# A PEER expert kernel on one core: gate blocks loaded in four parts, second top 16 over 64 sums, gathered rows summed at the head of a step

## The reference

```python
s = einsum('thpd,hpnd->thpn', q, sub_keys)            # 8 heads, 2 key halves, 128 keys each
sv, si = top_k(s, 16)                                 # first top 16, per token, head and half
cand = sv[:, :, 0, :, None] + sv[:, :, 1, None, :]    # 16 x 16 = 256 sums per token and head
cidx = si[:, :, 0, :, None] * 128 + si[:, :, 1, None, :]
top_s, pos = top_k(cand, 16)                          # second top 16
idx = take_along_axis(cidx, pos); gate = softmax(top_s)
act = gelu(x . u_tab[idx])                            # 128 experts per token (8 heads x 16)
out = sum_k gate * act * v_tab[idx]
```

## Time and profile before

| | |
|---|---|
| median of 3 runs | 4110.21 us (4100.69 to 4113.46) |
| the profiled execution | 4114.83 us, its span 4112.9 us |
| busy in the span | TensorE 3465.9 us (84%), VectorE 2977.0 us (72%), GpSimd 1071.2 us, ScalarE 996.2 us |
| chain that ended last | TensorE 47%, VectorE 20%, DMA 20%, issue 8%, ScalarE 3% |
| DMA | 1268.02 MB, mean 308 GB/s; in the slices of the 128 steps 359 to 414 GB/s, in the last slice 282 GB/s |
| largest groups | L1067 687.1 us, L1079 490.3 + 240.6 us (TensorE); L1686 462.3 + 307.6 us (VectorE) |

### The profile page before, as it was taken

How to read it: one execution, slowest core, us unless ns; L and a number is a source line. 1 busy time by engine, 2 the same in 40 slices (tenths; PEclk the granted TensorE clock), 3 DMA queues, 4 the chain that set the end, 5 groups by cost and what they waited for, 6 DMA issues and landing times.

```text
span 4112.9 us, 32147 instructions
## 1 busy us (share of the span) xinstructions
PE 3465.9 (84%) x9517; PEld 1750.2 (43%) x9517; DVE 2977.0 (72%) x6346; ACT 996.2 (24%) x2518; POOL 1071.2 (26%) x950
## 2 busy tenths in 40 slices
PE   6876899976779778667777698999899988999998
PEld 4336344432343344224445344444444444444443
DVE  1536797847637686798998777887787867876666
ACT  1212321345241111127668111111111111111111
POOL 0000222211213122332320233333233323333331
PEclk9988899987889889888886899999999999999999
DMA  5343665765757788898882899999999999999997
GB/s 201 135 158 134 232 233 212 273 225 208 266 223 276 281 294 318 307 374 329 322 317 107 359 393 383 395 393 402 368 405 392 414 368 363 386 412 390 403 400 282
DMA packets 254837, 1268.02 MB, mean 308 GB/s; under 512 B 24596, under 2 KB 75028, under 8 KB 135622
## 3 DMA queue, kind: packets, MB, share of 16 engines
q0 software_dynamic: 131504, 958.53, 59.1%
q1 hardware_dynamic: 121720, 302.19, 19.7%
q10 hardware_dynamic: 1440, 5.24, 0.3%
HBM read 1216.30 MB, written 49.58 MB: 308 GB/s over the span
## 4 chain that ended last, share of the span: by engine, by line
PE 47%; DVE 20%; DMA 20%; issue 8%; ACT 3%; POOL 1%; SPq 1%; DVEq 0%; POOLq 0%; ACTq 0%
PE bank L1067 8%; DMA arena<-in_uv 8%; PE wide L1079 7%; PE bank L1026 4%; PE bank L995 4%; PE bank L831 4%; DMA ring_e<-in_uv,idx 4%; PE bank L854 3%; PE bank L1079 3%; PE wide L786 3%; DMA arena<-in_uv,idx 3%; PE bank L978 3%; DVE arena L1686 2%; DMA arena<-in_w_q 2%; DVE arena L1740 2%
## 5 line engine op out<-in xcount | busy, mean ns | idle before, releaser
L732 POOL DMA_INDIRECT arena<-in_uv,idx x384 | 446.2, 1162 | 1066.9 <-PE bank L1026 657.9
L1067 PE MATMUL bank<-arena 128*128 128x384 f32 x2048 | 687.1, 489 | 29.7 <-ACT arena L1418 16.4
L1686 DVE CUSTOM_DVE_ANT_0 arena<-arena,h2e 128x1024 f32<-128x1024 f32 x384 | 462.3, 1222 | 235.5 <-DMA arena<-in_uv,idx 234.5
L708 POOL DMA_INDIRECT ring_e<-in_uv,idx x256 | 303.3, 1185 | 1077.8 <-PE wide L786 521.9
L1079 PE MATMUL wide<-arena 128*128 128x512 f32 x1024 | 490.3, 624 | 107.2 <-DMA arena<-in_uv 107.2
L1067 PEld LDWEIGHTS bank<-arena 128*128 128x128 f32 x2048 | 391.1, 191 | 332.1 <-issue 94.1
L732 POOL DMA_INDIRECT ring_e<-in_uv,idx x256 | 298.4, 1166 | 566.8 <-PE bank L1026 362.9
L1360 ACT ACTIVATE small<-small 128x4 f32<-128x4 f32 x160 | 32.9, 205 | 1692.8 <-DVE small L1686 1647.5
L1626 DVE CUSTOM_DVE_ANT_0 ring_e<-ring_e,h2e 128x1024 f32<-128x1024 f32 x256 | 307.7, 1222 | 166.4 <-DMA ring_e<-in_uv,idx 165.9
L1686 DVE CUSTOM_DVE_ANT_0 ring_e<-ring_e,h2e 128x1024 f32<-128x1024 f32 x256 | 307.6, 1221 | 125.8 <-DMA ring_e<-in_uv,idx 125.5
L1079 PEld LDWEIGHTS wide<-arena 128*128 128x128 f32 x1024 | 204.2, 201 | 375.1 <-issue 253.8
(11 more groups left out here) (248 smaller groups left out, 4766.4 us busy)
## 6 DMA issues: line engine op xcount, KB each, us to landing
arena<-in_ut SPq DMA_DIRECT2D x128, 512.0 KB
arena<-in_uv SPq DMA_DIRECT2D x128, 512.0 KB
arena<-in_w_q SPq DMA_DIRECT2D x48, 512.0 KB
spread_d<-arena SPq DMA_DIRECT2D x12, 2048.0 KB, 9.2
arena<-spread_d SPq DMA_DIRECT2D x32, 768.0 KB
ring_e<-in_w_mod POOLq DMA_DIRECT2D x8, 2048.0 KB, 8.2
arena<-in_w_cols SPq DMA_DIRECT2D x24, 512.0 KB
arena<-in_x SPq DMA_DIRECT2D x20, 512.0 KB, 5.6
```

The source lines that it names most:

```text
L708: pool.indirect_dma_start(out=ring_e[k % ERING], out_offset=None, in_=a["uv"], in_offset=bass.IndirectOffsetOnAxis(ap=idx[k // SLOTS][:, k ...
L732: pool.indirect_dma_start(out=ring[r], out_offset=None, in_=a["uv"], in_offset=bass.IndirectOffsetOnAxis(ap=idx[kept(t)][:, k:k + 1], axis ...
L1067: ins = pe.matmul(s_bank[:, 0:NC], lhsT=utb[i % URING][:, k * P:(k + 1) * P], rhs=H2T[1][:, k, P:P + NC], start=(k == 0), stop=(k == KD - 1))
L1686: dve.tensor_tensor_reduce(out=ring[r][:, 0:D], in0=ring[r][:, 0:D], in1=h2b[kept(t)], scale=1.0, scalar=0.0, op0=ALU.mult, op1=ALU.add, a ...
```

## The change

Three edits.

1. **Gate blocks in four parts.** `load_gates(gr, part)` loads 3 of the 12 groups (192 KB, 384 runs of 512 bytes). Where a block of four steps was one DMA in every fourth iteration, between `load_u` and `load_v`, each iteration now issues one quarter of the next block, behind `load_v`. The last quarter of block g is issued in iteration 4g-1; the first step that reads block g is 4g.
2. **Second top 16 over 64 sums.** The 16 best of 256 sums of two sorted lists lie in a staircase: row a of the first list needs at most 16/(a+1) columns. Four blocks of rows (1 x 16, 3 x 8, 4 x 4, 8 x 1) hold it in 64 sums. They are made for all 8 heads by four instructions ahead of the first head, and each head's five top-16 instructions run over 64 instead of 256 numbers. The way back from a position among 64 to row and column takes more arithmetic: the first `finish` step has 15 counted instructions instead of 5.
3. **TensorE's order in a step**: `sums_half`, `scores_of(i)`, `sum_rows(i-1)`, where it was `scores_of(i)`, `sums_half`, `sum_rows(i-1)`.

```diff
-            def load_gates(gr):
-                if gr >= GRING:
+            def load_gates(gr, part):
+                if gr >= GRING and part == 0:
                     sp.wait_ge(*S["w_ready"].at((gr - GRING + 1) * NG - 1))
-                dst = gwb[gr % GRING].rearrange("p (g i t) -> p g i t", i=NG, t=SPAN)
-                src = spread_d[:, :, gr * NG:(gr + 1) * NG, :].rearrange("g p i t -> p g i t")
+                c = slice(part * CN, (part + 1) * CN)
+                dst = gwb[gr % GRING].rearrange("p (g i t) -> p g i t", i=NG, t=SPAN)[:, c]
+                src = spread_d[c, :, gr * NG:(gr + 1) * NG, :].rearrange("g p i t -> p g i t")
                 sp.dma_start(dst, src).then_inc(*S[f"gw_in{gr % GRING}"].mark(gr, 16))
...
-            load_gates(0)
+            for part in range(NG):
+                load_gates(0, part)
...
                     load_u(i + 2)
-                if i % NG == 1 and i // NG + 1 < ETILES // NG:
-                    load_gates(i // NG + 1)
                 if i + 1 < ETILES:
                     load_v(i + 1)
+                if i // NG + 1 < ETILES // NG:
+                    load_gates(i // NG + 1, i % NG)
...
             for i in range(ETILES):
+                if i:
+                    sums_half(GROUPS_A + i - 1)
                 scores_of(i)
                 if i:
-                    sums_half(GROUPS_A + i - 1)
                     sum_rows(i - 1)
...
+                def stairs():
+                    v4 = sv.rearrange("p (h r a) -> p h r a", r=2, a=TOPK)
+                    c3 = cand.rearrange("p (h c) -> p h c", c=STAIR)
+                    at = 0
+                    for a0, rows, width in STAIR_ROWS:
+                        dst = c3[:, :, at:at + rows * width]
+                        va, vb = v4[:, :, 0, a0:a0 + rows], v4[:, :, 1, 0:width]
...
+                        done(dve.tensor_tensor(dst, va, vb, ALU.add))
+                        at += rows * width
                 def head(h):
                     after()
-                    cd = cand[h % 2]
-                    done(dve.tensor_tensor(cd.rearrange("p (a b) -> p a b", b=TOPK),
-                                           va.unsqueeze(2).to_broadcast([P, TOPK, TOPK]),
-                                           vb.unsqueeze(1).to_broadcast([P, TOPK, TOPK]), ALU.add))
+                    if h == 0:
+                        stairs()
                     after()
-                    top16(cd, ts[...], pos[...])
+                    top16(cand[:, h * STAIR:(h + 1) * STAIR], ts[...], pos[...])
...
+                def places():
+                    low, high, at, flat = (cand[:, i * SLOTS:(i + 1) * SLOTS] for i in range(4))
...
+                    done(dve.tensor_scalar(low, low, -1.0, 0.0, ALU.add, ALU.max))
+                    after()
+                    done(dve.scalar_tensor_tensor(out=high, in0=high, scalar=-6.0, in1=low, op0=ALU.add, op1=ALU.max))
...
+                    done(dve.tensor_tensor(at, low, high, ALU.min))
+                    after()
+                    done(dve.tensor_tensor(pf[1], flat, at, ALU.subtract))
...
-                        done(dve.tensor_scalar(pab[0], pos, 4, None, ALU.logical_shift_right))
-                        done(dve.tensor_scalar(pab[1], pos, 15, None, ALU.bitwise_and))
-                        after()
-                        for r in range(2):
-                            done(dve.tensor_copy(pf[r], pab[r]))
+                        places()
...
+STAIR = 64
+STAIR_ROWS = ((0, 1, 16), (1, 3, 8), (4, 4, 4), (8, 8, 1))
-FINISH = (5, 2, 2, 2, 4)
+FINISH = (15, 2, 2, 2, 4)
```

More of the change, by code:

```diff
@@ L249, in build @@
         fss, frs, gsum = (small[:, 6 * GROUP + i:6 * GROUP + j] for i, j in ((0, 5), (5, 10), (10, 10 + PH)))
-        cand = [sb(f"cand{i}", [P, TOPK * TOPK])[:] for i in range(2)]
+        cand = sb("cand", [P, PH * STAIR])[:]
         sv, sf = (sb(n, [P, HP * TOPK])[:] for n in ("sv", "sf"))
@@ L1480, in pick_step @@
                 scr, oneh = where
-                count = [5 * q if q < HP else 5 * HP + 6 * (q - HP) if q < HP + PH else
+                count = [5 * q if q <= HP else 5 * q + len(STAIR_ROWS) if q < HP + PH else
                          CHAIN - sum(FINISH[q - HP - PH:])]
@@ L1513, in keys @@
                           si[:, hp * TOPK:(hp + 1) * TOPK])
+                def stairs():
[5 more added lines that the diff above has]
+                        va, vb = v4[:, :, 0, a0:a0 + rows], v4[:, :, 1, 0:width]
+                        if rows > 1 and width > 1:
+                            dst = dst.rearrange("p h (a b) -> p h a b", b=width)
+                            shape = [P, PH, rows, width]
+                            va, vb = va.unsqueeze(3).to_broadcast(shape), vb.unsqueeze(2).to_broadcast(shape)
+                        else:
+                            shape = [P, PH, rows * width]
+                            va, vb = va.to_broadcast(shape), vb.to_broadcast(shape)
+                        done(dve.tensor_tensor(dst, va, vb, ALU.add))
+                        at += rows * width
                 def head(h):
                     after()
-                    va, vb = (sv[:, (2 * h + r) * TOPK:(2 * h + r + 1) * TOPK] for r in range(2))
-                    cd = cand[h % 2]
-                    done(dve.tensor_tensor(cd.rearrange("p (a b) -> p a b", b=TOPK),
-                                           va.unsqueeze(2).to_broadcast([P, TOPK, TOPK]),
-                                           vb.unsqueeze(1).to_broadcast([P, TOPK, TOPK]), ALU.add))
+                    if h == 0:
+                        stairs()
                     after()
-                    top16(cd, ts[:, h * TOPK:(h + 1) * TOPK], pos[:, h * TOPK:(h + 1) * TOPK])
+                    top16(cand[:, h * STAIR:(h + 1) * STAIR], ts[:, h * TOPK:(h + 1) * TOPK], pos[:, h * TOPK:(h + 1) * TOPK])
                 t3 = ts.rearrange("p (h k) -> p h k", k=TOPK)
@@ L1544, in sum_key @@
                     done(dve.tensor_reduce(pi[r], o3, AX.X, ALU.add))
+                def places():
+                    low, high, at, flat = (cand[:, i * SLOTS:(i + 1) * SLOTS] for i in range(4))
+                    done(dve.tensor_scalar(pab[0], pos, 3, None, ALU.logical_shift_right))
+                    done(dve.tensor_scalar(pab[1], pos, 2, None, ALU.logical_shift_right))
+                    done(dve.tensor_copy(flat, pos))
+                    after()
+                    done(dve.tensor_copy(low, pab[0]))
+                    done(dve.tensor_copy(high, pab[1]))
+                    after()
+                    done(dve.tensor_scalar(low, low, -1.0, 0.0, ALU.add, ALU.max))
+                    after()
+                    done(dve.scalar_tensor_tensor(out=high, in0=high, scalar=-6.0, in1=low, op0=ALU.add, op1=ALU.max))
+                    after()
+                    done(dve.scalar_tensor_tensor(out=pf[0], in0=flat, scalar=-48.0, in1=high, op0=ALU.add, op1=ALU.max))
+                    after()
+                    done(dve.tensor_scalar(low, pf[0], 8.0, 8.0, ALU.mult, ALU.min))
+                    done(dve.tensor_scalar(high, pf[0], 3.0, 24.0, ALU.mult, ALU.min))
+                    after()
+                    done(dve.scalar_tensor_tensor(out=low, in0=pf[0], scalar=8.0, in1=low, op0=ALU.mult, op1=ALU.add))
+                    done(dve.scalar_tensor_tensor(out=high, in0=high, scalar=24.0, in1=pf[0], op0=ALU.add, op1=ALU.add))
+                    after()
+                    done(dve.tensor_tensor(at, low, high, ALU.min))
+                    after()
+                    done(dve.tensor_tensor(pf[1], flat, at, ALU.subtract))
                 def finish(part):
@@ L1594, in pick_step @@
                     finish(q - HP - PH)
-                assert count[0] - n0 == (5 if q < HP else 6 if q < HP + PH else FINISH[q - HP - PH])
+                assert count[0] - n0 == (5 + len(STAIR_ROWS) * (q == HP) if q < HP + PH else FINISH[q - HP - PH])
             def early(s, phase, n):
@@ L2083, in _ @@
                 normalised(t, x1c[j], 2 + j)
-FINISH = (5, 2, 2, 2, 4)
-CHAIN = 5 * HP + 6 * PH + sum(FINISH)
+STAIR = 64
+STAIR_ROWS = ((0, 1, 16), (1, 3, 8), (4, 4, 4), (8, 8, 1))
+FINISH = (15, 2, 2, 2, 4)
+CHAIN = 5 * HP + len(STAIR_ROWS) + 5 * PH + sum(FINISH)
 PICK_STEPS = HP + PH + len(FINISH)
```

## The result

The changed kernel takes 4069.5 us (median of 4 runs, 4059.2 to 4073.0) against 4110.5: a ratio of 0.990, 95% interval 0.988 to 0.993. It is 41 us faster, where the forecast had 104. The profiled execution took 4070.8 us, with a span of 4068.8 against 4112.9.

A forecast was written before the change was run, and what follows sets the result against it. The prediction took TensorE as the bound, with the DMA engines nearly full at 0.97. Gains of 60 + 8 + 6 + 3 + 27 = 104 us took the profiled 4114.8 to 4010.8, or 4006 us as median; range 3960 to 4072.

The forecast's parts named there:

- Waits for v, edit 1: In the 128 steps: splitting gate blocks removes the cause of all 17 TensorE waits for v, up to 107.2 us.
- nothing new is waited for: In a step: sums moved to the head find their diagonal matrices ready; gain bounded by 0 and 88 us.
- the 60: In the 128 steps: the joint gain taken for split gate blocks and TensorE's new order, 60 us.
- an earlier restart of the gathers: In the steps: ring buffers come free 5.16 us earlier, so gathers restart 5 us sooner after a wait for v.
- The DMA floor: In the 128 steps: 692 MB at 411 GB/s, or scaling by DMA share, bounds the gain at 94 us.
- The rival of the late quarter: In the steps: a block's last gate quarter lands too late for weigh, costing 164 us, total 4123 us; chance 0.08.
- the waits only move: In the steps: full DMA engines make u, v or gathers late instead, steps stay 1784 us, total 4066 us; chance 0.17.
- Picks: Top-16 selection for the tiles: 8.0 us shorter per tile, yielding 44 us in all, none of it in the 128 steps.
- tile 0: Stretch from 385 to 440 us: its picks' chain runs through the heads on VectorE; gain 8 us.
- The beats: The 40 beats before the 128 steps, holding the picks of tiles 3 to 6: gain 27 us, 85% of 32.
- The two terms of tiles 1 and 2: Stretches 440 to 590 and 1590 to 1712 us: shorter picks gain 6 us and 3 us.
- The 192 us: Estimated cost of 96 added gate DMAs at 2 us fixed cost each, if none overlapped; not in the forecast sum.

The follow-up runs named there:

- e2: Only the gate blocks in four parts, against the kernel before: ratio 0.9898, steps 1765.4 us.
- e4: The changed kernel with TensorE's old order: ratio 0.9827 to the kernel before, steps 1767.2 us.
- e3: Only TensorE's new order, against the kernel before: ratio 1.0084, slower, steps 1869.6 us.
- e14: The changed kernel with a gate block in three parts, the last issued one step earlier, new order: ratio 0.9789 to the kernel before, steps 1758.9 us.
- e9: e4 with only the load of u issued later, after the sums of gathered rows: ratio 0.9853 to the kernel before, steps 1788.4 us.
- e5: The changed kernel with each step's gathers held until the scores of the step before: ratio 0.9891 to the kernel before, steps 1793.9 us.
- e6: e4 with a gate block in three parts, the last issued one step earlier: ratio 0.9787 to the kernel before, steps 1760.4 us.
- e15: The changed kernel run once more, unaltered: ratio 0.9897 to the kernel before, steps 1809.0 us.
- e1: Only the second top 16 over 64 sums, against the kernel before: ratio 0.9904, steps 1799.5 us.
- e7: e4 with gates laid out in DRAM so a quarter is 128 runs of 1.5 KB: 4007.9 us, ratio 0.9742 to the kernel before.
- e11: e7 with TensorE's new order: 3992.7 us, ratio 0.9711 to the kernel before, steps 1719.2 us.
- e12: e7's layout and old order, but whole gate blocks in 6 KB runs: 4003.4 us, ratio 0.9725 to the kernel before.
- e13: e12 with TensorE's new order: 4001.1 us, ratio 0.972 to the kernel before, steps 1710.4 us.
- e8: The changed kernel with only the first two gate blocks loaded, output not the reference's: ratio 0.959 to the kernel before, steps 1679.4 us.

## Why the forecast of 104 us was wrong

**Waits for v, edit 1: right.** All 17 are gone, the v issues take 0.33 us, and alone it is worth 49 us of steps (e2), 41 us of the time.

**The step that failed: edit 3, "nothing new is waited for".** The prediction gave this edit bounds of 0 to 88 us of gain, inside the 60. It measured -36 to -42 us of steps (e4 against the changed kernel and its repeat), and -55 without edit 1 (e3). I looked at the diagonal matrices, which are ready, and at `load_u` ("comes 2.6 us later but is wanted 2.6 us later too"). That holds: the waits for u fell. I didn't look at what is issued behind `load_u` and keeps its deadline, which is the gate block and v in e3, nor at VectorE, where `weigh` waits for the last gate part and the join stands behind it. The new waits are for `weigh`, 56.8 us in place of 36.1, and for the join, 31.2 in place of 9.6. Both are gone in e14, where the last part has a step more. Why the last part lands later in the new order, up to 30.7 us in place of 25.6, stays open: moving u alone doesn't do it (e9), and holding the gathers gives back 9 us (e5).

The gain reckoned on, an earlier restart of the gathers, came about: VectorE's waits for gathered rows fell from 360.0 us before (234.5 and 125.5 by buffers) to 178.8 with the first two edits (e4) and 39.8 with the third. It bought nothing, since VectorE then waited for gates. The sum of the steps is -47 (e4) + 36 = -11, where -60 stood.

**The DMA floor was mis-sized.** The 411 GB/s came from a stretch of eight steps. It has two gate blocks in it, which is the usual mix, but its share of 1.02 isn't held over 128 steps. Per share the rates agree: 411 at 1.02, 389 at 0.97 over the steps before, 399 and 400 at 1.00 in e4 and e6 all make 399 to 403 GB/s at a share of 1.00. So 94 us were never to be had from this change: e6, at a share of 1.00, shows 54. Only fewer gate bytes or longer runs bring 406 to 411 at that share.

**The rival of the late quarter: its mechanism, not its price.** Its lead of at most 20.0 us was near the 21.4 measured. It took 25.3 us for every last part, 5.3 us in each of 31 blocks, 164 us in all; the last parts took 18.8 us in the median (e15), and measured were 16 waits and 56.8 us. It went wrong in the sign because it was priced too high.

**The forecast of "the waits only move", 4066 us**, is nearest in time by luck, since it knows nothing of the 47 us that edit 1 gave and the 36 that edit 3 took. It is right in that TensorE's idle time only fell from 126 to 110 us, but wrong in its reason: the waits moved to the gates, at a share of 0.98, not to a full DMA.

**Picks: right in total, less so in the parts.** 39.5 us by e1's ratio, 44 forecast. The stretch to the first early slot gave 6.4 (8 forecast for tile 0). The beats gave 28.5 in the first pair (27 forecast), but 20.9 in e1; they take 571 to 576 us in the three kernels with the old picks and 547 to 555 in those with the new ones and short runs. The two terms of tiles 1 and 2 (9) can't be told apart: the middle stretch varies from 1253 to 1272 us with the old picks and from 1257 to 1274 with the new. The top 16 over 64 took 1.38 us (1.39 estimated) and the places of the finish 3.4 (3.5):

```profile
3033.21 0.22 DVE L1498 MAX8 ts<-cand 128x8 f32<-128x64 f32 x1
3034.59 0.54 DVE L1792 TENSOR_TENSOR arena<-arena 128x384 f32<-128x384 f32 x1
...
3044.28 0.22 DVE L1567 TENSOR_SCALAR pab<-pos 128x128 uint32<-128x128 uint32 x1
3047.37 0.29 DVE L1588 TENSOR_TENSOR pf<-cand 128x128 f32<-128x128 f32 x1
```

From the first MAX8 to the next other instruction is the head; from L1567 to the end of L1588 are the places.

**What stays open.** The steps of e1 are 14.7 us shorter than before though its picks there were costed at nothing, while e4's are no shorter than e2's; no run separates this. Of the order's cost e5 explains up to 9 us; why the last gate part lands later than in e4 is not shown.

## What to carry to other kernels

When an instruction is moved on an engine, follow the loads that its completion starts, and then the loads that stand behind those in the same queue: they keep their deadlines (e3). An experiment that moves one of these alone must be read by its waits, not by its time: e9 cost 21 us at another place than the change did. When a load holds up its queue, look at the length of its runs before its size; a layout with longer runs took 39 us off the steps where splitting could do no more. Take a bandwidth floor from a long stretch, divided by its share, not from the best one.

## What was not expected of the hardware

A transfer of 512-byte runs slows what shares the DMA engines even when it is spread evenly: at a share of 1.00 the steps moved 400 GB/s with such runs in three of four steps (e6), 407 to 409 with 1.5 KB runs (e7, e11), 409 to 411 with 6 KB (e12, e13).

The Trainium skill (DMA: Bandwidth & Descriptors, Why small descriptors are slow) puts a fixed cost of some 3 bus cycles on each packet, at 32 bytes a cycle. An estimate from that is 3 on 16 cycles, 19% for 512 bytes: 57 us would become 68. e6 against e8 has 81, so the direction agrees and the size is larger here.

The same page's advice (Bandwidth) to batch DMAs to 1 MiB shows little: quarters of 192 KB and whole blocks of 768 KB differ by 9 to 12 us of steps once the runs are long (e11 and e13, e7 and e12), near the spread of 6, and the run length differs there too. The 192 us that the prediction estimated from that page for 96 more DMAs did not come; it is a figure without overlap, and the page measured it on DMAs issued from GpSimd, where these are SyncE's.

In the case shown above a wait of 6.7 us was followed by a granted clock of 0.54, near the lower of the two levels (1.2 of 2.4 GHz), for 6.5 us, and the matmuls in it took 2.9 us longer. The amount varies: behind the waits of 4.68 and 15.04 us in the earlier trace rows the same eight matmuls took 6.28 and 5.24 us, which is 2.7 and 1.6 more than 3.60.
